# Modulation rows on VectorE, convolution one step earlier, output projection begun inside the last recurrence

## The reference

```python
mx = split((silu(c) @ w_mod + b_mod), 6)          # rows 0..5: shift, scale, gate, shift, scale, gate
px = split_proj(modulate(x, pre_mix_g, mx[0], mx[1]) @ w_in)    # q, f_fwd, f_bwd, v, g, a, b: 512 columns each
ox = bidirectional gated recurrence, 4 heads of 128, chunks of 64, started from the context's last state
a  = rms_norm_per_head(ox) * silu(g)              # 512 channels, "k" = 0..3 of the concatenation
b  = silu(layer_norm(depthwise_conv31(a_proj * sigmoid(b_proj)) + bias))   # 512 channels, k = 4..7
x  = x + mx[2] * rms_norm(concat(a, b) @ w_out, post_mix_g)
h  = modulate(x, pre_ffn_g, mx[3], mx[4])
x  = x + mx[5] * rms_norm((silu(h @ w_gate) * (h @ w_up)) @ w_down, post_ffn_g)   # 2816 hidden channels
```

## Time and profile before

| | us |
|---|---|
| median of 3 runs | 1518.48 (1516.36 to 1520.56) |
| the profiled execution's own time | 1520.63 |
| its span | 1518.80 |
| granted TensorE clock, mean | 0.962 |
| PE busy | 1418.0 |
| DVE busy | 734.6 |
| ACT busy | 372.4 |
| POOL busy | 338.0 |

### The profile page before, as it was taken

How to read it: one execution, slowest core, us unless ns; L and a number is a source line. 1 busy time by engine, 2 the same in 40 slices (tenths; PEclk the granted TensorE clock), 3 DMA queues, 4 the chain that set the end, 5 groups by cost and what they waited for, 6 DMA issues and landing times. The chain is left out here.

```text
span 1518.8 us, 17923 instructions
## 1 busy us (share of the span) xinstructions
PE 1418.0 (93%) x6837; PEld 1153.6 (76%) x6837; DVE 734.6 (48%) x1021; ACT 372.4 (25%) x555; POOL 338.0 (22%) x143
## 2 busy tenths in 40 slices
PE   6699999999999956987989999999999999999998
PEld 2588888888888833546878888888888888888876
DVE  1802487688688789367551132332313323132227
ACT  2521321322131242245342212111111111112022
POOL 1511111111111065221132322122212221222110
PEclk8799999999999977988999999999999999999999
DMA  9110100100000063413221211111111101110122
GB/s 369 50 42 28 42 28 29 42 28 28 28 28 28 32 232 103 161 46 121 83 70 56 83 56 32 51 56 55 37 46 55 55 28 55 55 55 28 42 111 111
DMA packets 92656, 101.95 MB, mean 67 GB/s; under 512 B 3118, under 2 KB 77091, under 8 KB 92610
## 3 DMA queue, kind: packets, MB, share of 16 engines
q1 hardware_dynamic: 92610, 101.32, 20.2%
HBM read 92.92 MB, written 8.39 MB: 67 GB/s over the span
## 5 line engine op out<-in xcount | busy, mean ns | idle before, releaser
L529 PE MATMUL bank<-hT,ringb 128*128 128x512 f32 (+1 forms) x768 | 162.1, 368 | 0.0
L529 PEld LDWEIGHTS bank<-hT,ringb 128*128 128x128 f32 x768 | 131.4, 190 | 21.9
L1640 DVE TENSOR_TENSOR y<-bank,y 128x512 f32<-128x512 f32 x144 | 99.5, 691 | 89.9 <-PE bank L529 89.3
L1617 DVE TENSOR_TENSOR mid<-bank,sgm 128x512 f32<-128x512 f32 x44 | 30.4, 692 | 223.0 <-ACT sgm L1120 223.0
L529 PE MATMUL bank<-morec,mid 128*128 128x512 f32 x480 | 134.8, 389 | 0.0
L529 PE MATMUL bank<-slotX,mid 128*128 128x512 f32 x480 | 134.8, 389 | 0.0
L1336 DVE SCALAR_TENSOR_TENSOR conv_sum<-cat,taps,conv_sum 128x784 f32<-128x784 f32 (+14 forms) x90 | 114.9, 1277 | 10.6 <-DVE conv_sum L1336 6.0
L1620 DVE TENSOR_TENSOR mid<-bank,mid 128x512 f32<-128x512 f32 x44 | 30.4, 691 | 172.9 <-PE bank L529 172.9
L529 PE MATMUL bank<-hT,ringa 128*128 128x512 f32 (+1 forms) x480 | 106.2, 379 | 2.1 <-POOL hT L1169 1.6
L529 PEld LDWEIGHTS bank<-slotX,mid 128*128 128x128 f32 x480 | 90.1, 188 | 18.7
L529 PEld LDWEIGHTS bank<-morec,mid 128*128 128x128 f32 x480 | 90.1, 188 | 18.7
(11 more groups left out here) (198 smaller groups left out, 2401.1 us busy)
## 6 DMA issues: line engine op xcount, KB each, us to landing
mraw<-in_w_mod SPq DMA_DIRECT2D x48, 512.0 KB, 6.4
raw<-in_ffn_w_gate SPq DMA_DIRECT2D x22, 512.0 KB, 3.7
raw<-in_ffn_w_up SPq DMA_DIRECT2D x22, 512.0 KB, 3.7
raw<-in_ffn_w_down SPq DMA_DIRECT2D x22, 512.0 KB, 3.3
ringinb<-in_w_in SPq DMA_DIRECT2D x12, 512.0 KB, 3.7
ringina<-in_w_in SPq DMA_DIRECT2D x8, 512.0 KB, 3.9
xst<-in_x SPq DMA_DIRECT2D x8, 512.0 KB, 14.6
ringinc<-in_w_in SPq DMA_DIRECT2D x8, 512.0 KB, 4.0
```

The source lines that it names most:

```text
L529: return pe.matmul(o, l, r, start=start, stop=stop, skip_group_check=True)
L1617: dve.tensor_tensor(mid32[:, hf, :], bank[2 * hf][:], sgm[:, hf, :], ALU.mult).then_inc(gu_part, 1)
L1640: ins = dve.tensor_tensor(y[:, t, sl], b[:], y[:, t, sl], ALU.add)
```

## The change

- `TILES` are in the order b, a, ff, fb, q, g, v, and the latent token tiles are prepared before the context tiles (`TORD`). The convolution of head s stands in step s itself: `take` writes the convolution's input to `conv_u`, `conv_start` (L1400) writes the middle tap to the result and 30 `conv_tap` (L1405) add the others in place. `TAPS_FIRST` places them in step 0 (units 8 to 19), `TAPS_AFTER` in steps 1 to 3 (units 4 to 19). The last recurrence has no taps.
- Modulation rows 2 to 5 are 32 `mod_chunk` on DVE in step 0 (128x1024 each, four after each of units 0 to 7), which multiply a block of `w_mod` by the conditioning value of each partition and accumulate in `macc`. PE adds over the partitions in 32 small matmuls (`mod_sum`), and DVE's four `mod_take` stand behind all its other work of step 0. PE waits for `mod_done` 6 before step 1. SP loads the blocks into a ring of six, each when the block before it in its place is used.
- In the last recurrence PE runs the list `TAIL` between the recurrence's parts (`TAIL_AT`), in a ring of three banks: LayerNorm's sums and variances, the partial sums of tiles 4 to 7 over k = 0, 1, 2, those of tiles 0 to 3 over all k but 3 (21 matmuls each for two halves), and the gate rows. ACT copies each to `part[t]`. DVE's LayerNorm pieces and POOL's low halves of the concatenation (11) and of `w_out` (8) are in there too.
- After it, `mix(t)` needs only k = 3 for tiles 0 to 3 (6 matmuls) and k = 3 to 7 for tiles 4 to 7 (30 matmuls); DVE adds the partial sum (`mix_add`). `turn2(t-4)` stands behind `mix(t)` for t = 4 to 7, and `turn2` of tiles 4 to 7 is between the first gate and up units.
- The FFN's weights are loaded straight into their six places, without the raw buffers; a place is loaded when its last reader has finished. Round 0 has no `down` and the second gate row's broadcast is in round 1.

The core of the diff:

```diff
--- before.py
+++ after.py
-TILES = [("ff", 512), ("fb", 1024), ("q", 0), ("g", 2048), ("b", 3072), ("a", 2560), ("v", 1536)]
+TILES = [("b", 3072), ("a", 2560), ("ff", 512), ("fb", 1024), ("q", 0), ("g", 2048), ("v", 1536)]
...
-TAPS_AFTER = [0, 0, 1, 1, 1, 1, 1, 1, 3, 3, 3, 3, 3, 3, 3, 3]
-
-DVE_TAPS_AFTER = [0, 0, 1, 1, 1, 1, 1, 1, 1, 1, 1, 1, 1]
-ACT_TAPS_AFTER = [2, 2, 2, 2, 2, 2, 2, 1, 1, 1, 1, 1]
-assert sum(TAPS_AFTER) == sum(DVE_TAPS_AFTER) + sum(ACT_TAPS_AFTER) == TAPS - 1
+CHUNKS_AFTER = [4, 4, 4, 4, 4, 4, 4, 4]
+TAPS_FIRST = [0, 0, 0, 0, 0, 0, 0, 0, 3, 3, 3, 3, 3, 3, 2, 2, 2, 2, 2, 2]
+TAPS_AFTER = [0, 0, 0, 0, 1, 1, 1, 1, 2, 2, 2, 2, 2, 2, 2, 2, 2, 3, 3, 2]
...
+WO_ORDER = [0, 1, 2, 4, 5, 6, 7, 3]
+EARLY = [0, 1, 2]
+TAIL = [("sum", 0), ("sum", 1), ("var", 0), ("part", 4, 0), ("part", 4, 1), ("part", 5, 0), ("var", 1),
+        ("part", 5, 1), ("part", 6, 0), ("part", 6, 1), ("part", 7, 0), ("part", 7, 1)]
+TAIL += [("full", t, n) for t in range(4) for n in range(2)] + [("gate", 0), ("gate", 1)]
+TAIL_BY = ["dve" if u[0] == "sum" else "act" for u in TAIL]
+TAIL_AT = [0, 0, 2, 2, 3, 3, 4, 4, 5, 5, 6, 6, 7, 8, 9, 9, 10, 10, 11, 11, 12, 12]
+TRING = 3
...
+            def load_chunk(c):
+
+                if c < NCH:
+                    sp.wait_ge(mod_full, 2 * KT)
+                else:
+                    sp.wait_ge(mod_used, c - NCH + 1)
+                sp.dma_start(mraw[:, CHUNK_AT[c % NCH], :], wm[MODS[2 + c // KT], c % KT]).then_inc(chunk_in[c % NCH], 16)
...
+            def mod_sum(n):
+
+                pe.wait_ge(mod_used, (n - 1) * KT)
+                for j in range(KT):
+                    ins = mm(bank[LBASE + n - 2][:, j:j + 1], macc[:, n - 2, j * P:(j + 1) * P], ones[:, 0:1], True, True)
+                ins.then_inc(mod_turned, 1)
...
+            for n in range(2, 6):
+                mod_sum(n)
+            pe.wait_ge(mod_done, 6)
...
+            for u in range(OUT_AT + 3):
+                for i in PE_STEPS[u]:
+                    use(HEADS - 1, i)
+                for i in range(len(TAIL)):
+                    if TAIL_AT[i] == u:
+                        tail(i)
...
+            def mix(t):
+
+
+                pe.wait_ge(last_lo, t // 4 + 1)
+                if t >= 2:
+                    pe.wait_ge(mix_sum, 2 * t - 2)
+                elif t == 1:
+                    pe.wait_ge(use_act, (HEADS + 1) * N_UACT)
+                    pe.wait_ge(use_dve, (HEADS + 1) * N_UDVE)
+                else:
+                    pe.wait_ge(tail_act, TAIL_BY.count("act"))
+                    pe.wait_ge(o_lo, KT)
+                ks = [3] if t < 4 else [3, 4, 5, 6, 7]
+                if t == 4:
+                    pe.wait_ge(cat_lo, len(EARLY) + len(CAT_ORDER))
+                for n in range(2):
+                    for k in ks:
+                        ins = mix_step(bank[(2 * t + n) % 4], t, n, k, k == ks[0], k == ks[-1])
+                    ins.then_inc(mix_full, 1)
...
+            for t in range(XT):
+                mix(t)
+                if t >= 4:
+                    turn2(t - 4)
...
+            def pe_round(n, par):
+                for pos in range(4):
+                    for j in range(2):
+                        gate_up(n, pos, j)
+                        if first(n) and pos < 2:
+                            turn2(4 + 2 * pos + j)
+                    if isinstance(n, int) and n == 1 and pos == 1:
+                        pe.wait_ge(h2_free, 2 * XT)
+                        gate_rows()
+                if isinstance(n, int) and n == 1:
+                    pe.wait_ge(g_done, 1)
+                if not first(n) and not last(n):
+                    down(n - 1, 1 - par)
...
-                        load_ffn(n + 1, gu_no(n + 1, j), (KT + 4 + j) % RAW, GU[j])
+                        if j % 2 == 0:
+                            sp.wait_ge(gu_full, n * 8 + (8 if first(n) else 2 * j + 4))
+                        load_ffn(j, n + 1, GU[j])
...
+            def mod_chunk(c):
+
+                dve.wait_ge(chunk_in[c % NCH], 16 * (c // NCH + 1))
+                n, k = c // KT, c % KT
+                src, w, acc = mraw[:, CHUNK_AT[c % NCH], :], silc[:, k, 0:1], macc[:, n, :]
+                if k == 0:
+                    ins = dve.tensor_scalar(acc, src, w, None, ALU.mult)
+                else:
+                    dve.wait_ge(mod_used, c)
+                    ins = dve.scalar_tensor_tensor(acc, src, w, acc, ALU.mult, ALU.add)
+                ins.then_inc(mod_used, 1)
...
+            def dve_body(s, rec, taps):
+
+                for u in range(NUNIT):
+                    take(s, u)
+                    if rec:
+                        rec_step(s - 1, u, 0)
+                    if UNITS[u][1:] == ("a", 1):
+                        conv_start(s)
+                    for n in taps_after(taps, u):
+                        conv_tap(s, n)
+                    if rec:
+                        rec_step(s - 1, u, 1)
...
+                        for c in taps_after(CHUNKS_AFTER, u):
+                            mod_chunk(c)
+                conv_end()
+
+            dve_body(0, False, TAPS_FIRST)
+            for n in range(2, 6):
+                mod_take(n)
...
+            for u in range(OUT_AT + 3):
+                rec_step(HEADS - 1, u, 0)
+                rec_step(HEADS - 1, u, 1)
+                if u == 1 or u == 2:
+                    centre(u - 1)
+                elif u == 4 or u == 6:
+                    rstds(u // 2 - 2)
+                    normed(u // 2 - 2)
+                elif u == 5 or u == 7:
+                    swish(u // 2 - 2)
+            for hf in range(2):
+                sl = slice(hf * BANK, (hf + 1) * BANK)
+                dve.wait_ge(last_hi, hf + 1)
+                dve.tensor_tensor(cat_lo_t[:, 3, sl], cat[:, 3, sl], cat_hi_t[:, 3, sl].bitcast(F32),
+                                  ALU.subtract).then_inc(last_lo, 1)
...
+            mix_add(0)
             for t in range(XT + 1):
                 if t < XT:
                     x1(t)
+                if t + 1 < XT:
+                    mix_add(t + 1)
                 if t >= 1:
                     h2(t - 1)
...
+                if t < XT:
+                    x2(t)
```

More of the change, by code:

```diff
@@ L831, in down_both @@
                     ins.then_inc(down_full, 1)
-            gate_up(0, 0, (0,))
-            turn2(XT - 1)
-            pe.wait_ge(g_done, 1)
-            gate_rows(1)
+            def pe_round(n, par):
+                for pos in range(4):
+                    for j in range(2):
+                        gate_up(n, pos, j)
[6 more added lines that the diff above has]
+                    pe.wait_ge(g_done, 1)
+                if not first(n) and not last(n):
+                    down(n - 1, 1 - par)
             ffn_rounds(pe, pe_round)
@@ L901, in evac @@
                     w = min(BANK, TOK - n * BANK)
-                    if u == 0 and not first(s):
+                    if kind == "ff" and n == 0 and not first(s):
                         act.wait_ge(q_ready, s * NK + (2 - NK))
@@ new lines, in tail_take, with takes @@
+            def tail_take(i):
+                u = TAIL[i]
+                act.wait_ge(tail_full, i + 1)
+                if u[0] == "gate":
+                    out = Gb[:, u[1] * BANK:(u[1] + 1) * BANK]
+                else:
+                    out = part[u[1]][:, u[2] * BANK:(u[2] + 1) * BANK]
+                act.activation(out, bank[i % TRING][:], ACT.Copy).then_inc(tail_act, 1)
+            def takes(*kinds):
+                for i, u in enumerate(TAIL):
+                    if u in kinds:
+                        tail_take(i)
@@ new lines, in _ @@
+            swish_sig(1)
+            takes(("part", 7, 0), ("part", 7, 1))
+            rec_act(7)
+            ln_parts(1)
+            rec_act(8)
+            takes(("full", 0, 0), ("full", 0, 1))
+            rec_act(9)
+            takes(("full", 1, 0), ("full", 1, 1))
+            rec_act(10)
+            takes(("full", 2, 0), ("full", 2, 1))
+            rec_act(11)
+            takes(("full", 3, 0), ("full", 3, 1))
+            rec_act(12)
+            takes(("gate", 0), ("gate", 1))
+            rec_act(13)
@@ L1114, in act_tile @@
[L1114 to L1123 removed]
+                act.wait_ge(slot_in[j], n * 16 + 16)
@@ L1344, in part_start @@
[L1344 to L1356 removed]
+                dve.sem_inc(conv_done, 1)
@@ L1489, in dve_body @@
-                    if level:
-                        rec_level(h, level, 1)
-                    elif OUTER_AT <= u < OUTER_AT + SCAN:
-                        rec_states(h, u - OUTER_AT)
-                    else:
-                        rec_out(h, u)
-                    if not gemm and u in MOD_TAKE:
-                        mod_take(MOD_TAKE[u])
-                    if gemm and u == len(TAPS_AFTER) - 1:
-                        conv_end(h)
-            for u in range(NUNIT):
-                take(0, u)
+                elif level:
+                    rec_level(h, level, part)
```

(23 more changed lines are left out.)

774 lines of the change are left out of this document (355 added, 419 removed).

## The result

The changed kernel takes 1554.59 us (median of 4 runs, 1552.37 to 1555.53), the kernel before 1519.52 in the same comparison: the ratio is 1.0232 with a 95% interval of 1.0211 to 1.0252. Forecast were 1537.5 in a range from 1496 to 1552. The direction was right, the loss of 19 was 35, and the time lies outside the range.

What follows compares the result with a forecast made beforehand. TensorE bounds the kernel, busy 1418.0 of 1518.8 us. Step 0 +24.1, steps 1 to 3 +4.2 and the last recurrence to round 1 −9.3 give +19.0 on 1520.63, 1539.6, or 1537.5 as median; range 1496 to 1552.

Steps and rivals of the forecast that it cites:

- steps 1 to 3: Head steps after step 0: +4.2 (bounds −8.2 and +10), old waits removed, late K added in steps 2 and 3.
- The wait for K: Starts of steps 2 and 3: TensorE waits 6.8 each, plus 1.9 of lower clock; K ready at 10.3 in last recurrence.
- Step 0: First head step: VectorE's list ends at 177.4, TensorE needs it at 153.3, so +24.1 (bounds +9.7 and +31).
- The sign that it named: End of step 0: a wait of TensorE for mod_done, near 24.
- GpSimd's losses: Step 0: eight GpSimd subtractions each stretch a VectorE operation by 1.8, 14.4 in all.
- the rival in which it costs step 0 nothing: Step 0: no loss to GpSimd, so +9.7 there and a time of 1523; chance 0.14.
- The last recurrence: Step 3's end to second FFN round: levels end near 88, first mix at 142, −9.3 (bounds −45 and +24).
- a chain that no other work shortens: Pass over token tiles: h2, x2, x1, mix_add, mix, turn2, about 17 a turn; first mix to first gate matmul 80.5.
- Round 0: First FFN round: 69.0 in sum, from matmuls, transpositions, late weight splits, a place's reload and slower clock.
- The rival in which the tail gives what it removes: Last recurrence onward: ACT and GpSimd never bind, first mix at 125, stretch 266, −40.5, time 1506; chance 0.28.
- The rival of the three banks: Last recurrence: 22 evacuations each cost PE one more microsecond, stretch at +13, time 1559; chance 0.06.
- The rounds: Round 1 to the end: +5.7, as PE waits for the gate row's copy (3.7) and makes it (2.0); later rounds unchanged.

Runs made afterwards that it cites:

- Experiment 1: Changed kernel with ScalarE splitting the high half of v's weight before the last g unit instead of behind it: 1535.99 us, ratio to before 1.0107.
- experiment 2: Kernel before with one added ScalarE wait, so v's weight is split only after TensorE finishes the last a unit: 1542.06 against 1519.70, ratio 1.0154.
- Experiment 4: Changed kernel with another TAPS_AFTER: three taps after units 8 to 15, two after 16, none after 17 to 19: 1523.18 us, ratio 1.0024.
- experiment 3: Changed kernel with TensorE transposing tile t-4 before it projects tile t, not behind it: 1523.56 us, ratio 1.0030.
- the four edits: Changed kernel with v's weight split first, transposition before projection, taps earlier and first-round FFN weight places reloaded earlier: 1464.73 us, ratio to before 0.9638.

## Why the prediction was wrong, step by step

**The step that failed: steps 1 to 3, +4.2 where +20.1 was measured.** It counted TensorE's waits for VectorE and put those that ScalarE's list would cause at nothing, without a reason. The change put `g` where `a` had stood, and with it an evacuation in front of the copy of v's weight. Experiment 1 takes it out and 18.6 us go; experiment 2 puts it into the kernel before and 22.4 come. Without this wait steps 1 to 3 take 377.3, where the forecast had 378.0, so the rest of that term was right. The kernel is then at 1536, where 1537.5 was forecast; that this comes so near is partly luck, since 5.4 too much in step 0 and 3.5 too little in the rounds nearly cancel. In step 0 the same wait (4.61) costs at most 0.5 (171.95 against 171.44), because VectorE ends there just as late. The forecast looked at what stands in front in the lists of VectorE and TensorE, not in that of ScalarE, whose order the table of tiles changes without a line of `act_body` being about it.

**The wait for K** was right: forecast 6.8 and 10.3, found 6.84, 6.70 and 10.53. Experiment 4 shows the cause, twelve taps behind the last product, by moving them. Its price was nearly right: 2 x (6.8 + 1.9) and 10.3 make 27.7, and the three cost 31.4; the sum left out a lower clock behind the last wait, which can be the rest (the 32 matmuls behind it take 6.42, and 3.84 in experiment 4's kernel).

**Step 0** was right in that VectorE's list reaches its end that late, and too large by 5.4. The sign that it named, a wait of TensorE for `mod_done` near 24, was not there: the wait is 0.55. TensorE used the time for the `ringb` wait, slower matmuls behind it, and 9.98 of small sums, which the forecast had not put into TensorE's list. Experiment 1 shows that VectorE alone sets the same end: without the `ringb` wait TensorE waits 8.24 and step 1 starts at 171.44.

GpSimd's losses came true, and the rival in which it costs step 0 nothing falls. A chunk that meets a subtraction takes 3.23 instead of 1.285; the third modulation row's chunks (least, median and longest, in ns):

```profile
L1358 DVE SCALAR_TENSOR_TENSOR macc<-mraw,silc,macc x7: 1283/1285/3229, 103.6 to 111.9; 128x1024 f32<-128x1024 f32 x7
```

The 28 chunks were busy for 44.0, which is 8.0 above 28 x 1.285, by the four subtractions that meet them, 2.0 each where I had 1.8. Three taps lose 5.6, the first chunk 0.6 and one of the gate rows 1.7: 15.9 in all, where 14.4 was forecast. What was mis-sized is the gap between dependent operations: 0.2 in the sum, but in step 0 seven chunks with one loss took 11.56, so (11.56 − 1.94)/7 − 1.285 = 0.09, and between the taps it is less. About 60 gaps that are each at least 0.1 shorter give 6 to 8. Against that the four `mod_take` took 3.7 instead of 1.6, with the loss of 1.7 and the wait of 0.73 in them; together this is about the missing 5.4.

The Trainium skill ("SBUF — State Buffer", "Who interferes with whom") has a VectorE instruction with two SBUF inputs contend with a GpSimd instruction that reads SBUF, and the trace agrees in that. The block for a whole instruction it states for the two-port modes. Read as a full block for these operations too, as the estimate in the prediction did, it is not what the rows show, since GpSimd's subtraction is stretched as well, from 2.39 to 3.0: both lose.

**The last recurrence** was right: the levels end at 88.1 (88), the first `mix` is at 143.6 (142), the pass takes 76.7 (80.5), a turn 16.3 (17). What the forecast called a chain that no other work shortens could be shortened by a swap of two calls, which it did not price: 31.0 us (experiment 3). Round 0 was 72.1 (69.0). The rival in which the tail gives what it removes did not come true. With the four edits the stretch from step 3's end to round 1 is 238.5, less than the 261 of that rival, but not by its way: the first `mix` is at 130, where the rival had 125, and the gain is the pass, 46.4 where the rival had 72. The rival of the three banks falls too: TensorE's only wait for a partial sum's copy is 2.1.

**The rounds** were +9.2 (+5.7): 3.6 for the wait on the gate row, 2.0 for making it, and the rest slower matmuls behind 7.43 and 3.57 of waits (12.77 for 48 that take 11.2).

The range ended at 1552, 2.6 under the result, because no bound of its terms stood for a wait on an engine that the sum had left out.

## What to carry to other kernels

When the order of tiles changes, go through every engine's list, also of the one that is 24% busy: what stands in front of each copy that TensorE needs, and does it wait for something new. A wait of a busy TensorE cost 1.3 to 1.9 times its length here (3.39 became 6.3, 11.8 became 22.4, 24.1 became 31.4), and the short ones the most for their length, so several short waits are worth more than the table of waits says. And before a chain is taken as given, ask which of two neighbouring calls on one engine is on it: a turn of 16.3 became 7.7 by their swap.

## What had not been expected of the hardware

The 32 sums over partitions, one column each, cost TensorE 9.98 us as 64 matmul records, 0.16 each, no matter that a column is all they make. A VectorE operation that meets GpSimd's subtraction is stretched by about 2 us, and the subtraction itself by 0.6. And the lower granted clock was a third of the whole gain: of the 92.3 us between the changed kernel and the one with four edits, 33.2 are the same 6709 matmuls at a higher clock.
